# Eight blocks of projection products moved between the narrow causal units of two attention stages

## What the reference computes

```python
def _mixer(h, w_in, ...):
    z = h @ w_in
    (a_u, a_b, a_c, d_q, d_k, d_v, d_qi, d_ki, d_wi,
     f_q, f_k, f_v, f_f, s_q, s_k, s_v, g) = _split(z, IN_SIZES)
    y_a = _short_conv(a_u, a_b, a_c, conv_w)
    y_d = _dsa(...)    # sparse attention, 4 heads, the keys picked by an indexer
    y_f = _fox(...)    # forgetting attention, 4 heads, causal
    y_s = _swa(...)    # sliding window of 128, 4 heads
    ys = jnp.stack([y_a, y_d, y_f, y_s], axis=2)
    proj = jnp.einsum('blnc,ncd->blnd', ys, w_branch)
    gates = jax.nn.sigmoid(g.reshape(bsz, L, N_BRANCH, D_MODEL))
    return jnp.sum(gates * proj, axis=2) @ w_o
```

## Time and profile before

| what | value |
|---|---|
| median of 3 runs | 1680.34 us (1680.1 to 1680.52) |
| profiled execution | 1682.17 us |
| its span, first to last instruction | 1680.4 us |
| PE busy | 1637.5 us, 97% |
| DVE, ACT, POOL busy | 1050.6, 610.7, 822.6 us |
| mean granted clock of TensorE | 0.996 |

### The profile page before, as it was taken

How to read it: one execution, slowest core, us unless ns; L and a number is a source line. 1 busy time by engine, 2 the same in 40 slices (tenths; PEclk the granted TensorE clock), 3 DMA queues, 4 the chain that set the end, 5 groups by cost and what they waited for, 6 DMA issues and landing times.

```text
span 1680.4 us, 22907 instructions
## 1 busy us (share of the span) xinstructions
PE 1637.5 (97%) x8008; PEld 1344.3 (80%) x8008; DVE 1050.6 (63%) x1766; ACT 610.7 (36%) x1153; POOL 822.6 (49%) x538
## 2 busy tenths in 40 slices
PE   6999999999999999999999999999999999999997
PEld 4877877778888888887888887888888888888886
DVE  7745985786999999366685446554354345345437
ACT  5543336482232222267224454223222322322323
POOL 2431131104356666520886145757556656755765
PEclk9999999999999999999999999999999999999998
DMA  9131131021111111422872330112012111201205
GB/s 353 39 88 38 57 101 44 32 70 32 47 47 47 47 47 44 154 57 82 282 269 90 137 125 26 63 50 75 25 52 73 50 50 50 75 25 50 75 30 208
DMA packets 37745, 138.90 MB, mean 83 GB/s; under 512 B 4656, under 2 KB 4784, under 8 KB 37680
## 3 DMA queue, kind: packets, MB, share of 16 engines
q1 hardware_dynamic: 35440, 130.70, 22.4%
q0 software_dynamic: 2240, 7.34, 1.9%
HBM read 118.10 MB, written 13.63 MB: 78 GB/s over the span
## 4 chain that ended last, share of the span: by engine, by line
PE 63%; issue 13%; POOL 12%; DVE 5%; ACT 3%; DMA 3%; DVEq 0%; POOLq 0%; SPq 0%; ACTq 0%
PE ps L716 18%; PE ps L718 18%; PE ps L717 18%; POOL w_t L1881 6%; PE ps L968 2%; PE ps L932 2%; DMA raw<-in_w_ffn 1%; PE ps L850 1%; POOL w_f L1896 1%; PE ps L851 1%; POOL slot_c L1881 1%; POOL raw L1899 1%; DVE region_a L2257 1%; POOL region_d L1905 1%; DVE region_a L2446 1%
## 5 line engine op out<-in xcount | busy, mean ns | idle before, releaser
L716 PE MATMUL ps<-h_t,w_t 128*128 128x512 f32 x1112 | 436.6, 393 | 1.3 <-ACT y_t L1293 1.2
L718 PE MATMUL ps<-h_t,w_t 128*128 128x512 f32 x1112 | 433.0, 389 | 0.0
L717 PE MATMUL ps<-h_t,w_t 128*128 128x512 f32 x1112 | 432.8, 389 | 0.0
L716 PEld LDWEIGHTS ps<-h_t,w_t 128*128 128x128 f32 x1112 | 208.9, 188 | 46.9 <-issue 2.1
L718 PEld LDWEIGHTS ps<-h_t,w_t 128*128 128x128 f32 x1112 | 208.7, 188 | 43.5
L717 PEld LDWEIGHTS ps<-h_t,w_t 128*128 128x128 f32 x1112 | 208.8, 188 | 43.3 <-issue 0.9
L1721 POOL TENSOR_TENSOR w_t<-raw,w_t 128x1280 fp32r<-128x1280 f32 (+1 forms) x50 | 142.3, 2845 | 191.8 <-ACT w_t L1280 191.4
L2461 DVE TENSOR_TENSOR y_f<-ps,y_f 128x512 f32<-128x512 f32 x120 | 80.7, 686 | 217.5 <-PE ps L718 217.5
L1881 POOL TENSOR_TENSOR w_t<-raw,w_t 128x512 fp32r<-128x512 f32 x80 | 110.1, 1381 | 137.2 <-ACT w_t L1609 137.0
L2130 DVE MAX8 top<-region_b 128x8 f32<-128x512 f32 (+5 forms) x192 | 159.2, 883 | 19.8 <-issue 19.1
L2133 DVE MATCH_REPLACE8 region_b<-top,region_b 128x512 f32<-128x512 f32 (+5 forms) x192 | 166.3, 876 | 0.0
(11 more groups left out here) (304 smaller groups left out, 3279.2 us busy)
## 6 DMA issues: line engine op xcount, KB each, us to landing
raw<-in_w_ffn SPq DMA_DIRECT2D x46, 512.0 KB, 4.1
raw<-in_w_gates SPq DMA_DIRECT2D x32, 640.0 KB, 3.9
region_b<-in_w_ada SPq DMA_DIRECT2D x33, 512.0 KB, 4.6
region_d<-in_w_ffn SPq DMA_DIRECT2D x20, 512.0 KB, 4.3
raw<-in_w_z SPq DMA_DIRECT2D x18, 512.0 KB, 3.5
region_a<-in_x SPq DMA_DIRECT2D x8, 512.0 KB, 14.9
h_f<-in_w_ada SPq DMA_DIRECT2D x8, 512.0 KB, 9.2
raw<-in_w_o SPq DMA_DIRECT2D x8, 512.0 KB, 3.5
```

Of the source, the lines that this page charges most:

```text
L716: pe.matmul(o, a_hi, m_hi, start=first, stop=False, skip_group_check=more)
L717: pe.matmul(o, a_hi, m_lo, start=False, stop=False, skip_group_check=more)
L718: return pe.matmul(o, a_lo, m_hi, start=False, stop=last, skip_group_check=more)
```

## The change

In the first forgetting stage, the half tile of T_SWA (eight blocks, bank 5) is no longer a piece of its own behind the last transposes: a new step `fill_narrow` puts one block ahead of `turn_out` and `turn` at the even heads of b = 2 and b = 1, and two at b = 0, that is four blocks; the other four stay where they were. In the sparse stage `fill_narrow` does the same at the heads 0 and 2: eight blocks in six places, which are the whole first half of T_GD (now in bank 5). The places at the end of that stage keep their number of blocks, so the second half of T_GD (bank 4) and the first half of T_GD + 1 (bank 6) are begun in the stage as well. T_GD + 1 is finished by `gate_second`: its second half goes to bank 7, then its projections. For this, T_GD + 1 must be split early: ACT's `split_hi` of it moves from behind the stage to the stage's fifth unit, and POOL's `split_lo`, whose place in POOL's order is the same, can follow it. No instruction is added or taken away.

```diff
-FILL = {3: (1, 2, 2, 2, 3, 2), 2: (1, 1, 1, 1, 0, 1), 0: (0,) * 6}
+FILL = ((0,) * 6, (1, 2, 2, 2, 3, 2))
+FILL_SPARSE = (1, 1, 1, 1, 0, 1)
...
-            def attention(u0, n, gate=None, halves=0):
+            def attention(u0, n, gate=None, banks=()):
...
-                    for _ in range(parts):
+                    for _ in range(2 * parts):
                         next(beside, None)
+
+                def fill_narrow(u):
+
+                    kind, b, h = units[u]
+                    if u0 != U_FOX + 2 * TT and narrow(u) and b < 3 and h % 2 == 0:
+                        for _ in range(1 if b else 2):
+                            next(beside, None)
...
                         logits(u + 2)
+                    fill_narrow(u)
                     if u > u0:
                         turn_out(u - 1)
                     turn(u)
...
                 if u0 == U_FOX:
-                    pe.wait_ge(s_lg, 2 * TT)
-                    z_half(T_SWA, 1, 5)
+                    fill(KT)
                 turn_out(end - 1)
...
+            def swa_half_beside():
+
+                c = slice(HALF, L)
+                pe.wait_ge(s_zf, 2 * T_SWA)
+                pe.wait_ge(s_z_lo, lo_halves(T_SWA - 1) + 2)
+                pe.wait_ge(s_lg, 2 * (TT - HALF // P))
+                for k in range(KT):
+                    w = slice(k * P, (k + 1) * P)
+                    mm = product(ps[:, 5, :], w_t[:, T_SWA % 2, 0, w], w_t[:, T_SWA % 2, 1, w], h_hi[:, k, c],
+                                 h_lo[:, k, c], k == 0, k == KT - 1)
+                    if k == KT - 1:
+                        mm.then_inc(s_z, 1)
+                    yield
...
-            attention(U_DSA, HEADS * TT, T_GD, 2)
+            attention(U_DSA, HEADS * TT, T_GD, (5, 4, 6))
...
             gate_first(T_GD, 0)
-            gate_tile(T_GD + 1, 0)
+            gate_second(T_GD + 1, 0)
...
-            attention(U_DSA, HEADS * TT)
-            gate_pairs_begun(T_GD, 6 * KT, KT // 2 - 1)
+            attention(U_DSA, HEADS * TT, T_GD)
+            gate_pairs_begun(T_GD, 6 * KT, KT // 2 - 1, (5, 4))
```

More of the change, by code:

```diff
@@ L970, in values @@
                 mm.then_inc(s_pv, 1)
-            def attention(u0, n, gate=None, halves=0):
+            def attention(u0, n, gate=None, banks=()):
                 end = u0 + n
-                beside, parts_at = gates_beside(gate, halves), FILL[halves]
+                beside, parts_at = gates_beside(gate, banks), FILL_SPARSE if u0 == U_DSA else FILL[bool(banks)]
+                if u0 == U_FOX:
+                    beside = swa_half_beside()
                 def fill(parts):
-                    for _ in range(parts):
+                    for _ in range(2 * parts):
                         next(beside, None)
+                def fill_narrow(u):
[3 more added lines that the diff above has]
+                            next(beside, None)
                 logits(u0)
@@ L1016, in gate_half, with gates_beside @@
                     yield k
-            def gates_beside(T0, halves):
-                for n in range(halves):
+            def gates_beside(T0, banks):
+                for n, bank in enumerate(banks):
                     if n % 2 == 0:
                         pe.wait_ge(s_w_lo, T0 + n // 2 + 1)
-                    for k in gate_half(4 + n, T0 + n // 2, n % 2):
-                        if k % 2:
-                            yield
+                    yield from gate_half(bank, T0 + n // 2, n % 2)
+            def swa_half_beside():
[10 more added lines that the diff above has]
+                    yield
             def gate_first(T, buf):
@@ L1053, in _ @@
             pe.wait_ge(s_lo_even, 32)
-            attention(U_FOX + 2 * TT, 2 * TT + TT, T_AFS, 3)
+            attention(U_FOX + 2 * TT, 2 * TT + TT, T_AFS, (4, 5, 6))
             for bank in range(2):
@@ L1474, in _, with gate_tile @@
             act.activation(y_hi(0), ya_back[:, :, :], ACT.Copy).then_inc(s_ya_hi, 1)
-            def gate_tile(T, m, i=0, halves=(0, 1), bank=0):
+            def gate_tile(T, m, i=0, halves=(0, 1), banks=(0, 1)):
                 for half in halves:
@@ L1480, in gate_tile @@
                     act.wait_ge(s_mix, i * 4 + (MIX0 + m + half))
-                    act.activation(sig, ps[:, bank + half, :], ACT.Sigmoid)
+                    act.activation(sig, ps[:, banks[half], :], ACT.Sigmoid)
                     act.activation(prj, ps[:, 2 + half, :], ACT.Copy).then_inc(s_zf, 1)
@@ L1504, in mix_hi, with gate_pairs_begun @@
                 act.activation(h_hi[:, dt], z[:, dt], ACT.Copy).then_inc(s_mix_hi, 1)
[L1506 to L1510, removed]
+            def gate_pairs_begun(T0, m0, n=KT // 2, first=(4, 5)):
+                gate_tile(T0, m0, banks=first)
                 split_hi(T0 + 2, n=GT)
-                gate_tile(T0 + 1, m0 + 2, bank=second)
+                gate_tile(T0 + 1, m0 + 2, banks=(6, 7))
                 gate_pairs(T0 + 2, m0 + 4, n - 1)
-            gate_pairs_begun(T_AFS, 0, second=6)
+            gate_pairs_begun(T_AFS, 0)
             act.activation(y_hi(0), y_s, ACT.Copy).then_inc(s_ys_hi, 1)
```

## The result

The changed kernel takes 1687.47 us (median of 6, 1686.4 to 1690.68) against 1680.43 us; the ratio is 1.0042, with a 95% interval of 1.0032 to 1.0052. The profiled execution took 1690.68 us with a span of 1688.8 us. The forecast of 1680.9 us, with 0.87 on no change that can be measured, is wrong: the loss is twice what it called the limit of measuring.

The account below looks back on a forecast made before the run. PE was taken to bound the kernel, busy for 1637.5 of 1680.4 us. First stage -0.7 and T_GD + 2's later start +1.25 (sparse gain lost) sum to +0.55 us, added to the median 1680.34: 1680.9 us, range 1680.0 to 1681.9.

Parts of the forecast that it names:

- First stage, the waits that go: First forgetting stage: inserted blocks remove 0.95 us of PE waits, three insertions cost 0.27; -0.7 us, bounds -0.4 to -1.0.
- The signal s_z of the half tile comes with the end of PE's work as before, and the stage behind it moves as a whole.: End of the first forgetting stage: the last four blocks stay, so everything behind shifts together; no extra cost in the sum.
- Sparse stage, the waits that go: Sparse stage's narrow units: about 1.8 us of waits removed, six insertions cost 0.5; -1.4 us, bounds -0.9 and -1.8.
- The moved split: T_GD + 1's split, now within the sparse stage: 0 on PE, bounds 0 and 0.8; one slowed DVE copy hidden, bound 1 us.
- `gate_first` later by 4.1 us: Behind the sparse stage: eight more blocks ahead of it move its start by +5.5 - 1.4 = +4.1 us, to 805.4.
- POOL is the one that ends last, and the load adds 0 to 0.5 us.: Ahead of T_GD + 2: POOL's work on T_GD, ending at 816.1, sets the weights' time, 819.1; PE waits 2.6 us.
- short-wait rival: At T_GD + 2: POOL, spared DVE's company, is done 1.4 us sooner, PE waits 1.2 us; 1679.4 us, chance 0.18.
- The rival with GpSimd disturbed throughout: Between `gate_first` and T_GD + 2: POOL's five operations meet DVE, PE waits 6.2 us; 1684.5 us, chance 0.07.
- Half clock: Behind a wait of 2.6 us at T_GD + 2, PE's clock may fall: +1.7 us, 1682.6 us, chance 0.14.
- No second wait at T_GD + 3: At T_GD + 3: POOL is 3.6 us later and PE 1.25, leaving 0.5 us of cover, so PE does not wait.

Follow-up runs that it names:

- the kernel before with the one load put off: The kernel before, with the load of T_GD + 2 behind six loads for the modulation instead of four; ratio 1.0029.
- the sparse stage alone: Changed kernel with the first forgetting stage taken back to the kernel before, so only the sparse stage is changed; ratio 1.0023.
- the run with two halves begun: Changed kernel with the first stage taken back and only the two halves of T_GD begun in the sparse stage, load not moved; ratio 1.0020.

## Why the forecast was wrong

- **First stage, the waits that go.** Right: -0.7 forecast, -1.0 measured, the edge of its bounds.
- **"The signal s_z of the half tile comes with the end of PE's work as before, and the stage behind it moves as a whole."** The first step that failed. The stage did not move as a whole: VectorE's subtraction came 1.0 us sooner, while GpSimd's first low part, which stands behind DMAs that wait for a step behind the inserted blocks, came 0.9 us later, so that the one ran into the other. I had the mechanism, with a row of it, and weighed it only at the split that the change moves. The list of what runs beside what at the end of the first stage would have shown that the subtraction had 0.15 us to the first low part and 0.7 us to the second. Cost: 3.4 to 4.6 us in four profiles, where +0 stood in the sum.
- **Sparse stage, the waits that go.** Right in kind, too small: -1.4 forecast, -1.9 measured, just outside the bounds.
- **The moved split.** Right: the differences at 488 and at 767 us agree within 0.02 us. GpSimd's low part stands at 746.62; a copy of VectorE behind it takes 0.94 us, hidden.
- **`gate_first` later by 4.1 us.** About right: GpSimd's first multiply starts 810.37 - 804.10 - 2.6 = 3.7 us later in the stage.
- **"POOL is the one that ends last, and the load adds 0 to 0.5 us."** The second step that failed. I let the queue drain where it doesn't: every reload waits for a step behind six or all eight of the inserted blocks, so that the last one is 3.7 us late in the stage (4.1 forecast), and nothing of this is won back; the four loads behind it take 10.48 us instead of 8.99. The load is 5.0 us late where I allowed less than 4.1, and GpSimd was done 1.4 us sooner than I had it (it began 0.4 us sooner, and its adds took 1.29 and 1.62 us instead of 1.62 and 2.32, near the short-wait rival). So the chain was load, high part, low part, and the low part itself took 3.93 us beside VectorE instead of 2.96. The wait was 5.7 us for a forecast 2.6. With the load in time it is 2.70 us. The rival with GpSimd disturbed throughout had a wait of this size (6.2 us), but not this reason: ahead of the low part GpSimd was less disturbed than before.
- **Half clock.** A rival at 0.14, with +1.7 us behind a wait of 2.6 us. It happened, but behind one of 5.7 us; behind the first matmul of T_GD + 2, 2.0 and 2.4 us more are lost in the two profiles.
- **No second wait at T_GD + 3.** Right for the changed kernel, because the first wait was so long; with the first wait gone it appears there.

What stays open: what part VectorE's first use and what part the landing of the loads has in the 1.5 us by which the four take longer. The use took 1.42 and 1.87 us in the two profiles of the changed kernel against 0.77 before; from issue to that use it was 8.2 to 8.7 us, but also 8.76 us in the kernel before with the one load put off, whose order is the same up to there, against 7.86. No run holds the two engines apart at this place. Open too is why profiles show more loss than the ratios: 9.9 and 8.5 us from 279 us to the end for the changed kernel against 7.0 us, and 4.8 us against 3.9 us for the sparse stage alone.

## What to carry to other kernels

Work that fills an engine's waits puts off every step behind it, and with it each DMA that waits for such a step, as in both stages here: follow the queue to the first load that the critical engine needs next, and move that load ahead of what can wait. When an engine gets faster in one place, list what the others do in that microsecond: VectorE and GpSimd, each on its own chain, can begin to meet where they did not, and 0.3 us of work then costs 4. A wait's name is the last link only; what the named engine itself waited for tells the cause.

## What the runs showed of the hardware

A short VectorE subtraction of two SBUF operands that starts inside a GpSimd TENSOR_TENSOR lasts until 0.15 us behind the end of that one, and through a second one that follows at once: 4.17 us for 0.29, in four profiles (4.15 to 4.22 us). In the run with two halves begun, where the first stage is as before, it began by chance 0.33 us ahead of the end of the first low part (293.75) and took 0.48 us. VectorE's MAX8 beside the same GpSimd instruction kept its 0.56 us (the kernel before, at 296.32), and its addition of a PSUM and an SBUF operand, begun 0.01 us behind the low part of the changed kernel (292.14), kept its 0.29 us. The Trainium skill (SBUF — State Buffer, "SBUF: two separate sides") has the shared port pair as a lock that is kept to the end of an instruction, and names the VectorE instructions that need it: those in a 2-port mode and, beside a GpSimd instruction that reads SBUF, those with two SBUF inputs. These rows agree, and in them a waiting VectorE also loses to GpSimd's next instruction.

The half clock follows the length of a wait only roughly. Behind 4.09 to 5.70 us it came in all five profiles, for about 6.7 us; behind 3.40 and 3.55 us for about 3.4 us; behind 2.70 us once, behind 3.17 us not; and behind the same 2.8 us at the second forgetting stage in two profiles of four. The wait of 3.0 us of the earlier trace rows stands in all seventeen profiles of this study, and the clock fell behind it in thirteen.
